# Output projection, router and last norm: modulation rows spread over the partitions by DMA through DRAM instead of by matmuls

## The reference, cut to what matters

```python
mod = (silu(c) @ ada_w + ada_b).reshape(.., 6, 1024)      # sh1, sc1, gt1, sh2, sc2, gt2
h   = rms_norm(x, pre_mix_g) * (1.0 + sc1) + sh1
mix = concat([conv_group(h), rwkv_group(h)]) @ w_out
x   = x + gt1 * rms_norm(mix, post_mix_g)
h2  = rms_norm(x, pre_ffn_g) * (1.0 + sc2) + sh2
logits = h2 @ router_w + router_b                         # top 4 of 32 experts
x   = x + gt2 * rms_norm(experts(h2), post_ffn_g)
```

## Time and profile before

| | us |
|---|---|
| median of 3 runs (lowest, highest) | 1267.4 (1264.35, 1269.01) |
| profiled execution, its own time | 1266.23 |
| profiled execution, span of the trace | 1264.4 |
| busy: PE / DVE / ACT / POOL | 1174.5 / 412.7 / 208.6 / 89.2 |
| DMA: bytes moved, mean rate over the span | 452.13 MB, 358 GB/s |
| granted TensorE clock, mean | 0.982 of full speed |

### The profile page before, as it was taken

How to read it: one execution, slowest core, us unless ns; L and a number is a source line. 1 busy time by engine, 2 the same in 40 slices (tenths; PEclk the granted TensorE clock), 3 DMA queues, 4 the chain that set the end, 5 groups by cost and what they waited for, 6 DMA issues and landing times.

```text
span 1264.4 us, 15271 instructions
## 1 busy us (share of the span) xinstructions
PE 1174.5 (93%) x6048; PEld 556.8 (44%) x6048; DVE 412.7 (33%) x940; ACT 208.6 (16%) x457; POOL 89.2 (7%) x118
## 2 busy tenths in 40 slices
PE   5999999999999999989999999999999999999996
PEld 2886787774534433333333333333433333333332
DVE  0598767764422121212121221212121221212123
ACT  2411333232301111010101011111101011110102
POOL 2002543330000000000000000000000000000001
PEclk8999999999999999999999999999999999999998
DMA  9900363308799999999999999999999999999994
GB/s 365 361 35 31 148 259 134 134 6 356 288 422 431 431 431 431 431 426 430 430 431 438 431 431 431 429 423 389 432 430 431 439 430 431 431 430 430 421 425 188
DMA packets 34329, 452.13 MB, mean 358 GB/s; under 512 B 4440, under 2 KB 4968, under 8 KB 13688
## 3 DMA queue, kind: packets, MB, share of 16 engines
q1 hardware_dynamic: 33504, 450.78, 84.7%
q0 software_dynamic: 480, 0.80, 0.2%
q10 hardware_dynamic: 312, 0.11, 0.0%
HBM read 450.37 MB, written 1.31 MB: 357 GB/s over the span
## 4 chain that ended last, share of the span: by engine, by line
PE 52%; DMA 42%; DVE 3%; issue 1%; ACT 1%; SPq 0%; DVEq 0%; ACTq 0%
DMA ring<-in_w_gu 40%; PE bank L537 23%; PE bank L571 5%; PE bank L654 4%; PE bank L861 2%; DMA ring<-in_ada_w 2%; PE bank L753 2%; PE bank L763 1%; PE bank L504 1%; PE bank L494 1%; PE bank L762 1%; PE bank L649 1%; PE bank L702 1%; PE bank L664 1%; PE bank L524 1%
## 5 line engine op out<-in xcount | busy, mean ns | idle before, releaser
L537 PE MATMUL bank<-ring,front 128*64 128x512 f32 x2048 | 466.8, 611 | 39.5 <-DMA ring<-in_w_gu 39.5
L537 PEld LDWEIGHTS bank<-ring,front 128*64 128x64 f32 x2048 | 145.5, 140 | 358.5 <-issue 286.5
L1333 DVE TENSOR_SCALAR front<-bank 128x512 f32<-128x512 f32 x32 | 22.1, 692 | 515.3 <-PE bank L537 515.3
L571 PE MATMUL bank<-front 128*64 128x512 f32 x512 | 115.1, 603 | 8.1 <-ACT front L985 8.1
L571 PE MATMUL bank<-ring,front 128*64 128x512 f32 x512 | 113.4, 595 | 5.2 <-ACT front L985 5.2
L977 ACT ACTIVATE front<-front 128x512 f32<-128x512 f32 x32 | 20.1, 630 | 521.9 <-DVE front L1333 521.9
L1356 DVE COPY front<-bank 64x512 f32<-64x512 f32 x32 | 21.9, 684 | 166.6 <-PE bank L571 166.6
L1292 POOL TENSOR_TENSOR front<-front 128x512 f32<-128x512 f32 x4 | 5.4, 1372 | 929.8 <-DVE front L1325 929.8
L571 PEld LDWEIGHTS bank<-front 128*64 128x64 f32 x512 | 35.8, 138 | 77.2 <-issue 65.2
L571 PEld LDWEIGHTS bank<-ring,front 128*64 128x64 f32 x512 | 36.4, 137 | 71.9 <-issue 71.4
L504 PE MATMUL bank<-front 128*128 128x512 f32 x136 | 62.9, 605 | 0.9 <-DVE front L1356 0.9
(11 more groups left out here) (259 smaller groups left out, 1048.7 us busy)
## 6 DMA issues: line engine op xcount, KB each, us to landing
ring<-in_w_gu SPq DMA_DIRECT2D x56, 4096.0 KB
ring<-in_w_down SPq DMA_DIRECT2D x32, 2048.0 KB, 20.2
front<-in_w_down SPq DMA_DIRECT2D x32, 2048.0 KB, 19.7
ring<-in_w_gu SPq DMA_DIRECT2D x15, 2048.0 KB
ring<-in_ada_w SPq DMA_DIRECT2D x24, 1024.0 KB, 11.0
ring<-in_w_in SPq DMA_DIRECT2D x5, 2048.0 KB, 20.1
ring<-in_w_out SPq DMA_DIRECT2D x1, 4096.0 KB, 13.3
front<-in_x SPq DMA_DIRECT2D x2, 1024.0 KB, 5.1
```

Of the source, the lines that this page charges most:

```text
L537: last = pe.matmul(ps[r][64 * hf:64 * hf + 64, :], xT[:, k, S * q:S * q + S], wgu[:, k, r * F + hf * 512:r * F + hf * 512 + 512], start=Fa ...
L571: last = pe.matmul(ps[2][64 * c:64 * c + 64, :], actT[:, m, 64 * hf:64 * hf + 64], wdn[q][hf][:, m, c * 512:(c + 1) * 512], start=(k == 0) ...
L1333: v.tensor_scalar(glu, ps[0], 7.0, None, ALU.min).then_inc(s["glu_ready"], 1)
```

## The change

The rows are written once from `mod` to a scratch in DRAM (`mod_rows`, four DMAs of 8 KB), and twelve DMAs of 256 KB issued by POOL read each row 128 times, once for each partition, into SBUF: `gtb`, `a2b`, `b2b`. Four more for gt2 are issued by SP after the last use of the first matrix' buffer, into that buffer. The matmuls that spread, ACT's copies, and PE's waits for them are gone; DVE and POOL wait for the transfers and read SBUF.

```diff
+        mod_rows = nc.dram_tensor("mod_rows", (4, G, 2, 512), FP32).ap()
...
+        at_a2 = top_ra + 1024
+        a2b = view(front[:, at_a2:at_a2 + 2048], "p (n d) -> p n d", n=4)
+        b2b = view(r_rk, "p (n d) -> p n d", n=4)
...
-        gt2s = [view(a, "p (c n) -> p c n", c=2) for a in (r_r, r_V)]
+        gt2b = view(ring[:, 0:2048], "p (n d) -> p n d", n=4)
...  (SP, after the loads of the last expert)
+                sp.wait_ge(s["gu_used"], (N // S) * (E * KC))
+            with sp.Else():
+                sp.wait_ge(s["gu_used"], E * KC)
+            for n in range(4):
+                sp.dma_start(gt2b[:, n, :], mod_rows[2 + n % 2, n // 2, 1].partition_broadcast(P)).then_inc(s["gt2b"], 16)
...  (PE, last pair)
-                    spread_to(pe, 1, 2, 1, (4, 5)).then_inc(s["gtb"], 1)
...
-                    else:
-                        pe.wait_ge(s["glu_ready"], n * 2 + 2)
-                        spread_to(pe, 1, 2, 0, (0, 7)).then_inc(s["gtb"], 1)
...
-            if last_pair:
-                pe.wait_ge(s["gt2b"], turn * 4 + 4)
...  (PE, output projection)
-            pe.wait_ge(s["mod"], 2)
-            pe.wait_ge(s["vt"], Q)
-            pe.wait_ge(s["bo"], Q)
-            pe.wait_ge(s["gn_std"], Q)
-            spread(0, 0, 4).then_inc(s["gtb"], 1)
             pe.wait_ge(s["gn_out"], Q)
             for k in range(Q, KC):
                 project(k, 0)
-            pe.wait_ge(s["gtb_ev"], 4)
-            spread(1, 0, 4).then_inc(s["a2b"], 1)
             for k in range(KC):
                 project(k, 1)
-                if k == Q - 1:
-                    pe.wait_ge(s["mul1"], 2)
-                    spread(0, 2, 0, (0,)).then_inc(s["b2b"], 1)
-
+
+            pe.wait_ge(s["mul1"], 2)
+            pe.wait_ge(s["vt"], Q)
+            pe.wait_ge(s["gn_cen"], Q)
             turn_h2(0)
-            pe.wait_ge(s["mul1"], 4)
-            spread(0, 2, 0, (1,)).then_inc(s["b2b"], 1)
-            keep_clock(1)
+            keep_clock(2)
             logits(0)
...  (ACT: the copies into gt2s, L987 to L991, and into gtb, L1125 to L1127, are removed)
...  (POOL)
+            def spread(to, b, j0, n, name):
+
+                g, c = divmod(n, 2)
+                po.dma_start(to[:, n, :], mod_rows[j0 + c, g, b].partition_broadcast(P)).then_inc(s[name], 16)
...
             po.wait_ge(s["y_mm"], 2 * Q)
+            po.wait_ge(s["mod"], 2)
+            for j in range(4):
+                po.dma_start(mod_rows[j], mod[32 * j:32 * j + G]).then_inc(s["gtb_ev"], 16)
+            po.wait_ge(s["gtb_ev"], 64)
+            for n in range(4):
+                spread(gtb, 0, 0, n, "gtb")
+            for n in range(4):
+                spread(a2b, 1, 0, n, "a2b")
+            po.wait_ge(s["bo"], Q)
+            for n in range(4):
+                spread(b2b, 0, 2, n, "b2b")
             for r in range(2):
                 po.dma_start(bgu[E * r:E * r + E, :], b_gu[:, r * F:(r + 1) * F]).then_inc(s["in_router"], 16)
...
-            po.wait_ge(s["gt2b"], 4)
+            po.wait_ge(s["gt2b"], 64)
...  (DVE)
-            v.wait_ge(s["gtb_ev"], 4)
+            v.wait_ge(s["gtb"], 64)
...
-                v.wait_ge(s["a2b"], 1)
+                v.wait_ge(s["a2b"], 64)
...
-                    v.tensor_tensor(h2n[:, g, cols], x1[:, g, cols], ps[4 + n], ALU.mult)
+                    v.tensor_tensor(h2n[:, g, cols], x1[:, g, cols], a2b[:, n, :], ALU.mult)
...
-                v.wait_ge(s["b2b"], g + 1)
+                v.wait_ge(s["b2b"], 64)
...
-                                           ps[n].rearrange("p (r k) -> p r k", k=KC), ALU.mult, ALU.add)
+                                           b2b[:, n, :].rearrange("p (r k) -> p r k", k=KC), ALU.mult, ALU.add)
```

More of the change, by code:

```diff
@@ L477, in _ @@
             sp.wait_ge(s["stored"], 96)
[L480 to L487, removed]
         def gather(pe, number):
@@ L842, in _ @@
                 last.then_inc(s["st_mm"], 1)
[L844 to L852, removed]
             norm_mean(Q - 1)
@@ L867, in keep_clock @@
                 for _ in range(count):
-                    pe.matmul(ps[1], ident, const[:, K_MASK:K_MASK + 512], start=True, stop=True)
+                    pe.matmul(ps[7], ident, const[:, K_MASK:K_MASK + 512], start=True, stop=True)
             def turn_h2(g):
@@ L986, in act_pair @@
                                  ACT.Copy).then_inc(s["actT_ready"], 1)
[L987 to L991, removed]
                 a.wait_ge(s["dn_used"], n * 16 + KC * (q + 1))
@@ L1124, in _ @@
             norm_std(Q - 1)
-            a.wait_ge(s["gtb"], 1)
-            for n in range(4):
-                a.activation(gtb[:, n, :], ps[4 + n], ACT.Copy).then_inc(s["gtb_ev"], 1)
             def take_h2T(g):
@@ L1291, in _ @@
                 po.wait_ge(s["y_sum"], n + 1)
-                po.tensor_tensor(scaled[:, g, cols], yacc[:, g, cols], gt2s[g][:, n % 2, :], ALU.mult).then_inc(s["mul1"], 1)
+                po.tensor_tensor(scaled[:, g, cols], yacc[:, g, cols], gt2b[:, n, :], ALU.mult).then_inc(s["mul1"], 1)
         def choose(v, i):
@@ L1648, in _ @@
                         .then_inc(s["x1"], 1)
-                v.wait_ge(s["a2b"], 1)
+                v.wait_ge(s["a2b"], 64)
                 for n, cols in two:
                     v.wait_ge(s["x1"], n + 1)
-                    v.tensor_tensor(h2n[:, g, cols], x1[:, g, cols], ps[4 + n], ALU.mult).then_inc(s["v_step"], v_at.mark("h2_1"))
+                    v.tensor_tensor(h2n[:, g, cols], x1[:, g, cols], a2b[:, n, :], ALU.mult).then_inc(s["v_step"], v_at.mark("h2_1"))
                     if n == 2 * g:
@@ L1664, in _ @@
                                            h2n[:, g, cols].rearrange("p (r k) -> p r k", k=KC), rs2[:, g:g + 1],
-                                           ps[n].rearrange("p (r k) -> p r k", k=KC), ALU.mult, ALU.add).then_inc(s["h2"], 1)
+                                           b2b[:, n, :].rearrange("p (r k) -> p r k", k=KC), ALU.mult, ALU.add).then_inc(s["h2"], 1)
             v.wait_ge(s["in_router"], 64)
```

## The result

The changed kernel takes 1289.5 us (median of 5 runs, 1288.1 to 1291.1) against 1267.4 before (5 runs, 1264.4 to 1269.9): a ratio of 1.0172, interval 1.0155 to 1.0189, or 22.1 us slower. Forecast were 1283.7, with a range of 1272 to 1293. The sign, the place and the mechanism were right; the size was 5.8 us short. The profiled executions took 1288.1 after and 1266.2 before, with spans of 1286.2 and 1264.4: +21.8, of which +16.3 were forecast.

A forecast was written before the change was run, and what follows sets the result against it. The expert stage, a DMA-bound full pipe of 900 us, was taken to start as late as its first load: +15.8 (sh2 late, PE's 4.9 gain inside) + 0.5 (clock) = +16.3 on 1266.2 gives 1282.5, median 1283.7; range 1272 to 1293.

The forecast's parts named there:

- The rule: Time moves as much as SP's first fine_gu issue (342.1 us), which opens the expert stage, a full pipe of 900 us.
- The part removed: Ten of twelve spreading matmuls between PE's projection slices stand in the chain of waits; removing them saves 4.90 us.
- How the engines share: On each DMA engine, POOL's and SP's queues take turns by packet, not byte; all twelve broadcasts take 60 turns.
- Rival (b): POOL's queue gets two packets to a turn, sh2 lands at about 326.5, +6.4: 1273.8 us; chance 0.13.
- Rival (a): Engines share by bytes or POOL's queue goes first; rows arrive in time, -4.9 us: 1262.5; chance 0.07.
- sh2's landing: Last broadcasts, on which DVE's g = 1 steps wait, land at about 336.5 us by bytes at 425 GB/s; +15.8 us.
- rival (c): Mixing queues costs DMA throughput from 293 to 336; sh2 lands at 347, +27 us: 1294, an upper end; chance 0.14.
- The writes: POOL's four writes of mod to DRAM: last issued at 288.7, landed at 291.5; twelve broadcasts issued by 297.6 us.
- Where the first two groups stand in the queue: gt1 lands at about 312 us and sc2 at about 324; their place does not matter to sh2's landing.
- The chain of g = 1: DVE finishes g = 0 2.02 us after sh2's landing, then runs g = 1's steps in 6.5 us, ending at 345.0.
- The clock: PE idles from 317.9 to 338.5 us and its granted clock falls: +0.5 us, bounds 0 and +4.
- The last pair: gt2's transfers at the end of the run are hidden and the L485 matmuls lie in a gap: 0, bounds 0 and +1.7.

The follow-up runs named there:

- e1: Changed kernel with SP's five early weight loads cut by columns into 4 KB and 2 KB rows, same bytes: 1271.5 us against 1268.4, ratio 1.002.
- e2: Changed kernel with SP waiting for all twelve broadcasts before it issues its loads of expert weights: 1274.6 us, ratio 1.0055.
- e9: Kernel before with sc2 and sh2 by DMA and SP's five early loads in short pieces: 1269.0 us against 1269.6, ratio 1.0001.
- e10: Changed kernel with the twelve broadcasts on SP's queue, ahead of its weight loads, with no wait between: 1272.5 us, ratio 1.0027.
- e5: Kernel before without the matmuls that spread sc2 and sh2, no transfer in their place, wrong factors used: 4077 us, a total that means nothing.
- e4: Changed kernel with 46 keep_clock matmuls added on PE before the turn of h2: 1300.7 us, ratio 1.0241.
- e6: Kernel before with gt2 alone by DMA, gt1, sc2 and sh2 still by matmuls: 1267.4 us against 1268.1, ratio 0.9993.
- e8: Kernel before with sc2 alone by DMA (two writes, four broadcasts, 1 MB): 1264.5 us against 1268.1, ratio 0.9981.
- e11: Changed kernel with SP's weight loads after the twelve transfers, each reading 128 different rows of w_out: 13.7 us for that stage, total not read.

## Why the prediction was right, and where its size was off

**The rule.** "The time moves by as much as that first issue moves": it moved by 23.8 us, the span by 21.8. The expert stage changed by -2.0, within what it differs by between kernels that leave SP's loads alone. In those whose early loads are cut short or held back (e1, e2, e9, e10), it got longer by 2.7 to 6.6. So the rule holds to 2 us for the change, but not for these. "Everything loaded before that is the same in both kernels" left out the rows' own 3.15 MB.

**The part removed.** 4.90 us on PE's path were claimed. sc2 and sh2 alone gave 3.3 (e5), and all three together 5.5 between `mod` and `h2` (e2, e10). Right, if 0.5 low.

**How the engines share.** Turns by packet, one for one: 45 to 45, 111 to 113. gt1's 20 turns took from about 302, the first of its packets, to 320.6, 18.6 us or 0.93 each, between the forecast's 1.4 and 0.8. The Trainium skill, DMA: Bandwidth & Descriptors, section Queues, rings and completion order, says that an engine goes round the queues that have work, packet by packet. The trace agrees with that, by the equal counts. Rival (b), two packets to a turn, is excluded by them (its own sum was 0.5 too high besides: 326.5 + 2.02 + 6.47 = 335.0). Rival (a), rows in time, was excluded with them, and its number, 1262.5, was too low: e1 nearly has the rows in time and takes 1271.5. The DMA engines' slack from 315 to 345 in the kernel before is 9.0 us (six stretches of 5 us, at shares of 0.60, 0.34, one full, 0.81, 0.98 and 0.47), more than the pause of 5.4 that the prediction called the only one, and the added 3.15 MB need 7.4 of it. That e1's expert stage is longer because little of it is left is argued.

**The step that failed: sh2's landing.** The prediction's sum by bytes gave 336.5, 49.4 after `mod`; it came 53.1 after `mod`, at about 343.2, so 3.7 us late. One stretch after the change has the whole loss (columns of the earlier trace rows):

```profile
293.00:343.30 50.30, 27.32 (x66) 12.16 (x64) 8.22 (x20) 5.61 (x16) 9.18 (x17) 0.80 0.97 385
```

At the assumed 425 GB/s the bytes of these 50.3 us need 45.6, which is 4.7 less. 0.9 of it the forecast had allowed for (335.6 to 336.5); the rest, 3.8, is what was missed. The bytes include some 0.3 MB of `bgu` and `b_down`, which POOL queued behind the rows, so the account is good to about 0.7 us. The loss lies in three places:
- The rate while the queues mix: 398 GB/s from 293 to 320, where 425 was assumed. That is 27 x 27 / 425 = 1.7 us, the small true part of rival (c).
- The rate of the short packets: from 335 to 340, with SP's load running out, 356 GB/s, or 0.8 us. It is the 355 of e2. (From 320 to 335 the rate was slightly above 425, which gives 0.3 back.)
- The end: 340.0 to 343.3 runs at 104 GB/s, bytes that need 0.8 us at the full rate, so this tail costs 2.5. A sum by bytes presumes that all 16 engines end together, and they don't: of sh2's 64 signals 45 are in by 340.0 and the last comes at 343.22. Of gt1's and sc2's last transfer, 15 of 16 are in by 319.6 and 338.0, and the last comes 1.1 and 1.2 us later.

Two more steps of the working were wrong, without moving that sum:
- The writes. The forecast had a small transfer land 2.8 us after its issue, so at 291.5, 4.4 after `mod`. They let POOL go at 298.79, 8.7 after `mod`, and its packets begin at about 302, 12 after `mod` and 6 later than forecast. The forecast had allowed for 2 ("nor does a POOL that is 2 us later"). Whether the late start lengthened the tail is open: no run changed the start alone.
- Where the first two groups stand in the queue. gt1's 312 should read 313.8 by its own terms (305 + 11 x 0.8). sc2's 324 leaves out that its last eight turns meet the eight 32 KB packets of `load_gu(0, 1)`, at 1.4 us each: about 334. The trace bears that out, with 60 packets of SP's queue, 1.97 MB, beside 61 of POOL's, 0.20 MB, from 330 to 335. So it was sc2 and not sh2 that shared with that load. Against these numbers, and with `mod`'s 3.0 taken off, gt1 came 3.8 and sc2 2.2 late.

The 9.2 us that the prediction works out for twelve transfers on engines with nothing else to do is not borne out either: e2 took 13.9.

**The chain of g = 1** took 8.55 from 343.30, forecast 2.02 + 6.47 = 8.49. **The clock** was +1.1 for +0.5, within its bounds; e4 confirms the number. As forecast, most of the slow stretch lay beside DVE's chain: the clock is 0.50 from 345.4 to 350 and 0.97 from 350 to 354, and `h2` ends at 351.85. **The last pair** was 0, as forecast (e6; in the changed kernel POOL's product stands at 1276.29, released by L1306).

**The sum.** 16.3 forecast + 3.9 (`mod` to `h2`) + 0.6 (clock) + 3.0 (before `mod`, not of the change) - 2.0 (expert stage) = 21.8.

## What to carry to other kernels

Here the queues of a DMA engine shared by packet: small rows queued beside long contiguous loads got the ratio of the packet sizes, a fifth of the bytes beside packets of 16 KB and under a tenth beside 32 KB, so a small transfer that something waits for needs short packets beside it, or an empty engine. Ahead of a stage that is bound by a full pipe, count the pauses of the pipe (9 us here) before adding traffic: in the traces 1 MB fit (e8), 2 MB gave back what they won (e9), and 3 MB lost (e1). A few microseconds of matmul between other matmuls are a cheap way to spread a row; before replacing them, price what the replacement queues behind.

## What the runs showed of the hardware beyond that

- Four 8 KB writes to DRAM took 8.1 us from the first issue to the release of the waiting engine (7.7 in e2, 7.6 in e11, where no weight load ran beside them), two took 2.8 (e8). It is the fourth that is late: after the change the first three land 2.0 to 3.9 us after their issue and the fourth 6.3, at 298.5, just as SP's 1 MB load of x does, which was issued 0.4 us before it and lands at 298.8. e8, with only two writes, issues both ahead of that load. That the load holds up the fourth write is likely and was not tried.
- Twelve 256 KB broadcasts took 13.9 us on POOL's queue with no weight load beside them, 13.7 from different rows, and 15.5 on SP's queue with weight loads behind them, where 3.15 MB at 425 GB/s need 7.4. The repeated row is not the cause, nor POOL's queue alone. In e2, 3.15 MB at the 355 GB/s of its busy stretch would take 8.9; the rest is the slow first 3 us and the end, where the engines finish one after the other.
- PE idle for about 1 us of 3, amid small work, was followed by clock 0.50 for some 9 us and cost 3.9 us (e2, e10). The 25 us of idleness after the change cost only 1.1. There the clock was back before `h2` ended; in e2 it fell at about 329, right as `h2` ended at 329.3, and all of it lay on the path. Why 1 us of idleness was enough in e2 stays open.
- The clock dips to 0.72 to 0.97 between 190 and 245 us in some executions and not in others of the same code, while the end of the early part moves by up to 7.5 us from profile to profile. Differences of a few microseconds between totals are therefore better read from the table's later columns.
